# A table's value stage on one core: 1152 of 2048 columns multiplied whole instead of 1068, and 26 of 64 slabs as three split products

## The reference, cut to what matters

```python
best, pos = lax.top_k(cand, PEER_TOPK)              # 16 experts for each of 8 heads: 128 per token
expert = jnp.take_along_axis(cand_idx, pos, axis=-1)
gates = jax.nn.softmax(best, axis=-1)
u_sel = u_tab[expert]                               # tables of 16384 rows x 2048 columns
v_sel = v_tab[expert]
act = jax.nn.gelu(jnp.einsum('td,thkd->thk', xb, u_sel))
out = jnp.einsum('thk,thkd->td', gates * act, v_sel)
...
x = x + out
return rmsnorm(x, norm_final)
```

## Time and profile before

| | us |
|---|---|
| median of 3 runs | 2338.94 (2338.73 to 2341.91) |
| the profiled execution's own time | 2338.41 |
| its span, first to last instruction | 2336.6 |
| TensorE busy | 2275.4 |
| VectorE busy | 1754.7 |
| ScalarE busy | 745.3 |
| GpSimd busy | 755.0 |
| mean granted clock | 0.995 |

### The profile page before, as it was taken

One profiled execution on the slowest core, in us unless ns is written; L12 is line 12 of the kernel. 1 busy time (PEld: TensorE's weight loads), 2 busy tenths in 40 slices (PEclk: granted clock), 3 DMA queues, 4 the chain that ended last, 5 costly groups with the idle time before them and its releaser, 6 DMA issues.

```text
span 2336.6 us, 31490 instructions
## 1 busy us (share of the span) xinstructions
PE 2275.4 (97%) x12458; PEld 2085.6 (89%) x12458; DVE 1754.7 (75%) x3356; ACT 745.3 (32%) x1021; POOL 755.0 (32%) x664
## 2 busy tenths in 40 slices
PE   9999999999999999999999999999977899999997
PEld 7888888889999998998988888888877899999997
DVE  8666777668999897665698898566699866666666
ACT  4345556544345443444111111111375400000001
POOL 0000000000000000000475745656438766666674
PEclk9999999999999999999999999999999999999999
DMA  6554444545854544556798999999832399999998
GB/s 222 189 181 170 171 163 163 198 171 176 248 181 164 180 163 143 182 206 231 273 407 312 413 404 345 401 412 413 322 136 75 123 418 418 418 418 418 416 418 327
DMA packets 112499, 630.28 MB, mean 270 GB/s; under 512 B 14688, under 2 KB 15968, under 8 KB 69984
## 3 DMA queue, kind: packets, MB, share of 16 engines
q1 hardware_dynamic: 53712, 357.92, 40.8%
q0 software_dynamic: 58352, 270.04, 30.0%
q10 hardware_dynamic: 288, 0.31, 0.0%
HBM read 623.95 MB, written 4.26 MB: 269 GB/s over the span
## 4 chain that ended last, share of the span: by engine, by line
PE 90%; DVE 7%; DMA 1%; ACT 1%; issue 1%; ACTq 0%; DVEq 0%
PE ps L1152 19%; PE ps L1104 19%; PE ps L794 14%; PE ps L797 7%; PE ps L748 6%; PE ps L771 5%; PE ps L778 5%; PE ps L772 5%; PE ps L1063 4%; DVE ps L2293 2%; DVE work L2333 2%; PE ps L1117 1%; PE ps L1144 1%; DVE work L2318 1%; PE ps L1075 1%
## 5 line engine op out<-in xcount | busy, mean ns | idle before, releaser
L1152 PE MATMUL ps<-weight_raw,pairs 128*128 128x356 f32 x1536 | 462.8, 464 | 2.5 <-DMA weight_raw<-in_peer_v_dense 1.8
L1152 PEld LDWEIGHTS ps<-weight_raw,pairs 128*128 128x128 f32 x1536 | 454.1, 296 | 10.7 <-DMA weight_raw<-in_peer_v_dense 2.3
L1104 PE MATMUL ps<-work,weight_raw 128*128 128x256 f32 x2048 | 442.5, 379 | 0.0
L1104 PEld LDWEIGHTS ps<-work,weight_raw 128*128 128x128 f32 x2048 | 388.9, 190 | 52.8
L2347 DVE SCALAR_TENSOR_TENSOR scan_ws<-work,weight_raw,scan_ws 128x980 f32<-128x980 f32 x253 | 313.7, 1240 | 156.3 <-DMA work<-in_peer_v_rows,weight_raw 143.5
L1780 DVE TENSOR_TENSOR weight_low<-weight_raw,weight_high 128x2048 fp32r<-128x2048 f32 x145 | 332.2, 2291 | 102.1 <-ACT weight_high L1258 102.0
L693 POOL DMA_INDIRECT work<-in_peer_v_rows,weight_raw x255 | 315.0, 1235 | 166.3 <-DVE scan_ws L2347 109.6
L794 PE MATMUL ps<-operand_parts,weight_high 128*128 128x512 f32 x1456 | 354.9, 396 | 3.4 <-DVE slots L1766 1.2
L794 PEld LDWEIGHTS ps<-operand_parts,weight_high 128*128 128x128 f32 x1456 | 268.8, 188 | 61.1 <-issue 7.5
L1258 ACT ACTIVATE weight_high<-weight_raw 128x2048 fp32r<-128x2048 f32 x145 | 277.0, 1910 | 76.6 <-PE ps L797 71.0
L2284 DVE SCALAR_TENSOR_TENSOR work<-work,scan_ws 128x1024 f32<-128x1024 f32 x184 | 221.9, 1225 | 98.3 <-DMA work<-in_peer_u_rows,weight_raw 87.0
(11 more groups left out here) (299 smaller groups left out, 2670.0 us busy)
## 6 DMA issues: line engine op xcount, KB each, us to landing
weight_raw<-in_w_in SPq DMA_DIRECT2D x120, 1024.0 KB, 4.8
weight_raw<-in_peer_v_dense SPq DMA_DIRECT2D x64, 1068.0 KB
weight_raw<-in_peer_u_dense SPq DMA_DIRECT2D x64, 1024.0 KB
weight_raw<-in_w_out SPq DMA_DIRECT2D x32, 1024.0 KB, 4.8
weight_raw<-in_peer_w_q SPq DMA_DIRECT2D x13, 1024.0 KB
weight_raw<-in_conv_w_out SPq DMA_DIRECT2D x8, 1024.0 KB, 5.0
weight_raw<-in_ssm_w_val SPq DMA_DIRECT2D x8, 1024.0 KB
weight_raw<-in_ssm_w_gate SPq DMA_DIRECT2D x8, 1024.0 KB, 4.8
```

The lines of the kernel that those rows point to most:

```text
L1104: mm = nc.tensor.matmul(ps[:, 6 + s % 2, h * T:(h + 1) * T], w[:, h, k, :], gained_u[:, k, :], start=(k == 0), stop=(k == KU - 1))
L1152: mm = nc.tensor.matmul(ps_v[:, t, c, :], pairs[:, i // QKEYS, t * P:(t + 1) * P, i % QKEYS], w[:, i % 2, c * CW:(c + 1) * CW], start=(i = ...
```

## The change

The columns that are multiplied whole become 3 x 384 = 1152, and 896 are gathered. In 26 of the 64 slabs (SPLIT_VALUES: between slab 18 and slab 60, the first, second and fourth of every five) slab and placed weights are split into high and low parts, and TensorE makes three products of float32r operands. ScalarE copies the slab's two columns of `pairs` (512 elements in a partition) and the slab (2304 elements) to the high parts; VectorE subtracts both to get the low parts, at the rows given by LOW_AT. The new buffers lie in quarter 0 of `pairs` and below it. So what lay in quarters 0 and 1 moves up by one, and with it every step that waits for them: the residual is read back behind slab 35, the gain is spread ahead of slabs 36 and 38, the residual's transposes stand ahead of slabs 40 and 52, and VectorE adds them after rows 172 and 216. The buffers of picks and weights behind the slabs are laid out anew, because three slabs now cover 6912 elements.

```diff
@@ -40,7 +40,7 @@
 
 KU = 8
 UG = D - KU * P
-CBANKS, CW = 3, 356
+CBANKS, CW = 3, 384
 CV = CBANKS * CW
 VG = D - CV
 VH = VG // 2
@@ -109,8 +109,10 @@
 
     return max((e for e in range(g) if e in slot_of and slot_of[e] == slot_of[g]), default=None)
 DRAIN_SLABS = 3
-ADD_AT = (PICKS - 1, PICKS + 72)
-RESIDUAL_AT = (CLAIM + 8, 3 * CLAIM)
+ADD_AT = (PICKS + 44, PICKS + 88)
+RESIDUAL_AT = (2 * CLAIM + 8, 3 * CLAIM + 4)
+SPLIT_VALUES = [s for s in range(CLAIM + 2, PAIR_SLABS - DRAIN_SLABS) if (s - CLAIM - 2) % 5 in (0, 1, 3)]
+LOW_AT = {87 + (367 * (s - CLAIM - 3)) // 100: k for k, s in enumerate(SPLIT_VALUES)}
 PARTS = [slice(c * CW, (c + 1) * CW) for c in range(CBANKS)] + [slice(CV + c * VH, CV + (c + 1) * VH) for c in range(2)]
 
 
@@ -355,12 +357,17 @@
 
 
         keep = w_raw[:, NSLAB - 1, :]
-        gates, dots, pick_w = keep[:, 0:256], keep[:, 256:512], keep[:, 768:1024]
-        picks = keep[:, 512:768].bitcast(U32)
-        first_t, second_t = keep[:, 1024:1280], keep[:, 1280:1536]
-        whole_t, weight_t = keep[:, 1536:1792], keep[:, 1792:2048]
+        gates, dots, whole_t = keep[:, 0:256], keep[:, 256:512], keep[:, 512:768]
+        picks = keep[:, 768:1024].bitcast(U32)
+        pick_w, weight_t = keep[:, 1024:1280], keep[:, 1792:2048]
+        first_t, second_t = keep[:, 1280:1536], keep[:, 1536:1792]
         w_flat = w_raw[:, :, :].rearrange("p a n -> p (a n)")
         v_slabs = [w_flat[:, 2 * CV * n:2 * CV * (n + 1)] for n in range(RING)]
+        low_flat = w_low[:, :, :].rearrange("p a n -> p (a n)")
+        v_lows = [low_flat[:, 2 * CV * n:2 * CV * (n + 1)] for n in range(RING)]
+        parts_f = o_parts[:, :, :, :].rearrange("p a k t -> p (a k t)")
+        v_highs = [parts_f[:, 2 * CV * n:2 * CV * (n + 1)] for n in range(2)]
+        pair_parts = [parts_f[:, 4 * CV + 4 * T * n:4 * CV + 4 * T * (n + 1)].rearrange("p (x h t) -> p x h t", x=2, h=2) for n in range(2)]
         iota_key = lam_f[:, :, :].rearrange("p a b -> p (a b)")
         iota16 = iota_key[:, 0:PEER_K]
 
@@ -381,10 +388,10 @@
 
 
         pairs_f = pairs[:, :, :, :].rearrange("p q t i -> p (q t i)")
-        x_back = pairs_f[:, 0:4096].rearrange("p (k t) -> p k t", k=KD)
-        gain_diag, gain_b = pairs_f[:, 4096:6144], pairs_f[:, 6144:8192]
-        y_out = pairs_f[:, 8192:12288].rearrange("p (t n) -> p t n", t=TT)
-        out_junk = pairs_f[:, 12288:16384]
+        x_back = pairs_f[:, 8192:12288].rearrange("p (k t) -> p k t", k=KD)
+        gain_diag, gain_b = pairs_f[:, 12288:14336], pairs_f[:, 14336:16384]
+        y_out = pairs_f[:, 16384:20480].rearrange("p (t n) -> p t n", t=TT)
+        out_junk = pairs_f[:, 20480:24576]
         junk_v = out_junk[:, 2 * VG:2 * VG + TT * CV].rearrange("p (t c n) -> p t c n", t=TT, c=CBANKS)
 
 
@@ -504,6 +511,13 @@
                 M_S.append(M_B + 4 + len(M_TOK) + len(M_S))
 
 
+        HIGHS_BEFORE, LOWS_BEFORE = len(SPLIT_SLABS), len(SPLIT_SLABS) - len(LOW_BY_DMA)
+
+        def pairs_of(s):
+
+            i = 2 * (s % CLAIM)
+            return pairs[:, s // CLAIM, :, i:i + 2].rearrange("p t i -> p i t")
+
         block = ctx.enter_context(nc.Block())
 
 
@@ -607,9 +621,9 @@
                 else:
                     sp.wait_ge(v_done, s - RING + 1)
                 sp.dma_start(v_slabs[s % RING], d["peer_v_dense"][s]).then_inc(raw_landed[s % RING], 16)
-                if s == CLAIM + RING:
+                if s == 2 * CLAIM + RING:
                     sp.wait_ge(x_kept, 16)
-                    sp.dma_start(pairs_f[:, 0:4096], d["x_kept"]).then_inc(x_back_in, 16)
+                    sp.dma_start(pairs_f[:, 8192:12288], d["x_kept"]).then_inc(x_back_in, 16)
 
             def store(t, part):
 
@@ -1153,6 +1167,25 @@
                                           start=(i == 0), stop=(i == KEYS - 1), skip_group_check=True)
                 return mm
 
+            def split_values(k, s):
+
+                high, low = (x.rearrange("p (h n) -> p h n", h=2) for x in (v_highs[k % 2], v_lows[s % RING]))
+                pe.wait_ge(w_high_ready, HIGHS_BEFORE + 2 * k + 2)
+                pe.wait_ge(w_low_ready, LOWS_BEFORE + 2 * k + 1)
+                for h in range(2):
+                    for t in range(TT):
+                        for part in range(2):
+                            for c in range(CBANKS):
+                                nc.tensor.matmul(ps_v[:, t, c, :], pair_parts[k % 2][:, part, h, t * P:(t + 1) * P], high[:, h, c * CW:(c + 1) * CW],
+                                                 start=False, stop=False, skip_group_check=True)
+                pe.wait_ge(w_low_ready, LOWS_BEFORE + 2 * k + 2)
+                for h in range(2):
+                    for t in range(TT):
+                        for c in range(CBANKS):
+                            mm = nc.tensor.matmul(ps_v[:, t, c, :], pair_parts[k % 2][:, 0, h, t * P:(t + 1) * P], low[:, h, c * CW:(c + 1) * CW],
+                                                  start=False, stop=False, skip_group_check=True)
+                return mm
+
             def value_landed(s):
 
                 pe.wait_ge(raw_landed[s % RING], value_count(s))
@@ -1232,14 +1265,17 @@
 
             pe.wait_ge(pair_copied, TT * GROUPS_T)
             for s in range(PAIR_SLABS - DRAIN_SLABS):
-                if s in (CLAIM + 4, CLAIM + 6):
-                    spread_gain((s - CLAIM - 4) // 2)
+                if s in (2 * CLAIM + 4, 2 * CLAIM + 6):
+                    spread_gain((s - 2 * CLAIM - 4) // 2)
                 elif s in RESIDUAL_AT:
                     residual_tokens(RESIDUAL_AT.index(s))
-                value_landed(s)
-                for h in range(2):
-                    for t in range(TT):
-                        mm = value_tile(2 * s + h, t)
+                if s in SPLIT_VALUES:
+                    mm = split_values(SPLIT_VALUES.index(s), s)
+                else:
+                    value_landed(s)
+                    for h in range(2):
+                        for t in range(TT):
+                            mm = value_tile(2 * s + h, t)
                 mm.then_inc(v_done, 1)
             for t in range(TT):
                 for s in range(PAIR_SLABS - DRAIN_SLABS, PAIR_SLABS):
@@ -1692,15 +1728,34 @@
                     acted_relu(ACTED.index(g + 4))
 
 
-            act.wait_ge(v_done, CLAIM + 1)
-            for k in range(KD):
-                nc.scalar.activation(gain_diag[:, k * P:(k + 1) * P], ident[:, :], ACT.Copy,
-                                     scale=params[:, C_FINAL + k:C_FINAL + k + 1]).then_inc(gain_turned, 1)
-            for c in range(4):
+            def turn_gain():
+
+                act.wait_ge(v_done, 2 * CLAIM)
+                for k in range(KD):
+                    nc.scalar.activation(gain_diag[:, k * P:(k + 1) * P], ident[:, :], ACT.Copy,
+                                         scale=params[:, C_FINAL + k:C_FINAL + k + 1]).then_inc(gain_turned, 1)
+
+            def gain_out(c):
+
                 act.wait_ge(gain_spread, c + 1)
                 act_copy(gain_b[:, c * 512:(c + 1) * 512], ps[:, 6 + c % 2, :]).then_inc(gain_ready, 1)
+
+            for k, s in enumerate(SPLIT_VALUES):
+                act.wait_ge(v_done, SPLIT_VALUES[k - 2] + 1 if k >= 2 else CLAIM)
+                act_copy(pair_parts[k % 2][:, 0, :, :], pairs_of(s)).then_inc(w_high_ready, 1)
+                act.wait_ge(raw_landed[s % RING], value_count(s))
+                act_copy(v_highs[k % 2], v_slabs[s % RING]).then_inc(w_high_ready, 1)
+                following = SPLIT_VALUES[k + 1] if k + 1 < len(SPLIT_VALUES) else PAIR_SLABS
+                if s <= 2 * CLAIM + 1 < following:
+                    turn_gain()
+                if s <= 2 * CLAIM + 6 < following:
+                    gain_out(0)
+                    gain_out(1)
+                if s <= 2 * CLAIM + 8 < following:
+                    gain_out(2)
+                    gain_out(3)
             nc.scalar.activation(small[:, 52:53], eps_c, ACT.Sqrt)
-            act.wait_ge(v_done, 2 * CLAIM)
+            act.wait_ge(v_done, 3 * CLAIM)
             act.wait_ge(y_ready, 1)
             nc.scalar.activation(out_junk[:, 0:VG], y_tok[:, 0, :], ACT.Square, accum_out=out_cols[:, 0, CBANKS:CBANKS + 1]).then_inc(out_squared, 1)
             for t in range(TT):
@@ -2347,6 +2402,14 @@
                     v.scalar_tensor_tensor(out=y_tok[:, t, :], in0=row_at(s)[:, 0:VG], scalar=pick_w[:, g:g + 1], in1=y_tok[:, t, :],
                                            op0=ALU.mult, op1=ALU.add).then_inc(row_free[b], 1)
                 dve.wait_ge(row_free[b], USES[s] + 1)
+
+            def split_values(k):
+
+                s = SPLIT_VALUES[k]
+                dve.wait_ge(w_high_ready, HIGHS_BEFORE + 2 * k + 1)
+                v.tensor_tensor(pair_parts[k % 2][:, 1, :, :], pairs_of(s), pair_parts[k % 2][:, 0, :, :], ALU.subtract).then_inc(w_low_ready, 1)
+                dve.wait_ge(w_high_ready, HIGHS_BEFORE + 2 * k + 2)
```

(3 more changed lines are left out.)

## The result

The changed kernel takes 2344.82 us (median of 20 runs, 2338.04 to 2361.53), the kernel before 2338.05 (20 runs, 2331.44 to 2344.51). The ratio is 1.0034, 95% interval 1.0021 to 1.0046: **slower by 0.34%**, some 8 us by the ratio (the two medians lie 6.8 us apart). The forecast was a change too small to see (-1.8 us).

What follows compares the result with a forecast made beforehand. TensorE's pace was taken as the bound, transfers a few us behind, VectorE holding the last 15 us. Terms summed to -1.8 us: 2336.6 against the profiled 2338.41, or 2337.1 as a median; range 2329 to 2348.

Steps and rivals of the forecast that it cites:

- Products: TensorE's products in table two's 64 slabs: 457.5 us instead of 460.2, saving 2.7 us, with split records at 174.1 ns.
- Rival (b): Much faster, chance 0.05: a 384-column split record on TensorE takes 162.9 ns, products save 13.2 us, total 2322 to 2327.
- Residual blocks: TensorE's two blocks of residual transposes: 32 records instead of 40 in each, saving 1.8 us in all.
- Tail: After the first token tile's last product: VectorE's nine remaining row additions get shorter; the end gains 1.6 us.
- Slab 63: The last slab: TensorE waits 1.6 us for its landing instead of 1.8, a gain of 0.2 us.
- Slab 36: Split slab queued behind the kept residual's read on SP's queue: TensorE waits 3.5 us for it.
- For all split slabs but one I put 1.0 us in sum: TensorE's new waits before split slabs, slab 36 apart: 1.0 us together, at least nothing, at most 13 us.
- The transfers: DMA of slabs and gathered rows: 192.9 MB instead of 198.4, 13.2 us less at 418 GB/s, cover rather than gain.
- the last ten of the 40 slices: Reading of the profile before: the DMA engines are almost full in these slices, the stage of table two.
- Rival (c): Slower, chance 0.20: VectorE bounds the split stretch; TensorE stands 0.5 us at each of 26 splits, total 2350 us.
- GB/s falls below 418 in the split stretch: Expected sign in the profile: the DMA rate drops below 418 GB/s where slabs are split.
- the rows end some 3 us behind TensorE: Expected sign at the end of the kernel: VectorE's row additions finish some 3 us after TensorE.

## Why the prediction was wrong, point by point

- **Products** (-2.7 us): right. A record of 384 columns of the split type starts 173.3 ns after the one before it (2073.36 to 2077.52, 24 records), forecast 174.1 between the two neighbours; -2.3 us were measured. Rival (b) with 162.9 ns is out. The Trainium skill (TensorE: Matmul & The Clock Gate, Back-to-back issue gap) gives columns/2.4 + 2.5 ns for an isolated matmul, 162.5 ns here; the 173.3 ns measured in this stream do not agree with that figure.
- **Residual blocks** (-1.8): right, 3.57 us each. **Tail** (-1.6): right, -1.9. **Slab 63** (-0.2): right, -0.4 (1.43 us of wait instead of 1.6).
- **Slab 36** (+3.5): 3.44 us, but for a partly different reason. 1.5 us of it were the slab's landing and copy (the high part was ready at 2126.2, TensorE was there at 2124.65), the rest VectorE, whose subtraction ran from 2126.92 on. The other runs give VectorE less: seven rows earlier 2.10 us of the wait are left, and four rows later it is 2.15, both ended by ScalarE's copy. The step also left out the 1.3 us at the lower clock.
- **"For all split slabs but one I put 1.0 us in sum"**: this is the step that failed. It measured 10.3 us, and 1.3 at the lower clock. I had found 82 rows for a subtraction that stands behind row 83, called that "one short", and then gave a row that is not there no price, although its own bytes give one: 81 rows in 139.5 us are 1.7 us until the next (1.65 measured). With that price, the three rows that were missing besides are 5 us. Two of these three rows were missing because I carried the 418 GB/s of before over to other widths without putting a bound on it; the widening alone shows 412 and the same 79 rows. All other terms together came out at -3.0 us (forecast -2.8); these 10.3 us and the lower clock behind two waits (2.6 us, for which the sum had no term) turn that into +9.8. The range did hold the result, but only since it took in up to 13 us here for small waits at many slabs, which is not what happened; the likeliest value and the sign were wrong.
- **The transfers** ("need less and are no longer level with TensorE", 13.2 us of cover): not borne out. That price took 418 GB/s for both widths. At 412 GB/s the 192.9 MB are 6 us less than the 198.4 MB at 418, and over 1847 to 2310 us the share is 0.99 in the changed kernel and 1.00 with five rows earlier. The reading "the last ten of the 40 slices" should be the last eight, and TensorE reached slab 20 of the kernel before after 23.3 us (three slabs of 7.19 and a spread of 1.7), not 23.1; neither moves the sum.
- **Rival (c)** was VectorE as the bound of the whole split stretch, with waits at most split slabs. That did not happen in the changed kernel: 20 of 26 had none, and with the measured 3.62 us a split VectorE needs 32.3 of the 34.3 us that TensorE takes for five slabs. But VectorE's queue set the end of the versions with 356 and 376 columns, so the mechanism was named rightly and put at the wrong point. Its hold on GpSimd's requests is real: one takes 3.1 to 3.3 us beside a subtraction (1994.96 above), where it takes 0.95 alone. The Trainium skill (SBUF — State Buffer, on the shared port pair) states such a lock, held for the whole instruction, between a VectorE operation with two SBUF inputs and a GpSimd operation that reads SBUF. The trace agrees: that request ends at 1998.2, 0.8 us after the subtraction.
- **"GB/s falls below 418 in the split stretch"** (363 to 413 in stretches of 50 us) and "the rows end some 3 us behind TensorE" (2338.4 against 2335.9) were right, the first for another reason: the rate is at 412 before the first split.

What stays open: why 384 columns transfer at 412 GB/s and 376 at 420, why it falls to 404 late in the changed kernel, what cost the third missing row, and why the clock falls after some short waits and not after others.

## What to carry to other kernels

Where one engine's order is written by hand across two streams (here gathered rows and split slabs), compute at each fixed place how many items will have arrived, and charge every missing one at the pace of its arrival; a bound resource that is "level" gives that pace. When two resources are full at once, relieving one moves the bound to the third queue in line, so sum the work of every engine for the new kernel, VectorE's too, before expecting anything. And place such steps a little early rather than late: with 384 columns, 79 rows were there when TensorE came, and a first place behind row 78 or 75 gave the same time, while one behind row 87 instead of 83 cost TensorE 6.6 us more at that slab. That has an end too: with 376 columns and early places VectorE stood 29 us before high parts and its rows ended late.

## What the runs showed of the hardware that I had not expected

- The transfers' rate differs with the widths of rows and slabs with nothing else changed in kind. At full DMA share in 1870 to 1970 us, ahead of any split: 418 GB/s with gathered rows of 3920 bytes and slab rows of 8544; 420 with 3680 and 9024; 415 with 3632 and 9120; 412 with 3584 and 9216, in nine kernels with and without splits later on. It is not monotonic in either, and it is not the chip: 420, 415 and 412 were all taken on one.
- A wait of TensorE costs more than itself when the clock falls. The first 24 split records after a wait took 5.4 to 6.8 us, at a mean granted clock of 0.62 to 0.74, instead of 4.1 to 4.4 at 1.00 (356 to 384 columns), after waits of 14.30, 9.81, 7.75, 7.22, 4.94, 3.44, 3.30 and 3.13 us, but also after 2.40, 2.20, 2.10 and 2.04 (the last with four records of a gain spread between), while after 2.97, 2.71, 2.30, 2.15 and another of 2.04 they took 4.1 to 4.4. The length of the wait alone does not say it.
- The subtraction and the copy of 512 elements that are 32 apart take 1074 ns on VectorE and 1125 ns on ScalarE. In the kernel before, 490 to 512 elements side by side take VectorE 715 to 724 ns and ScalarE 598 (copies from PSUM). The operations differ in more than the step.
